# Order of the first loads, of the first panel's split and of the third panel's high part at the start of a two-block transformer kernel

## The reference, cut to what matters

```python
x = x + 0.5 * swiglu(rms_norm(x, norm_ffn1), ffn1_w1, ffn1_w3, ffn1_w2)

def swiglu(h, w1, w3, w2):
    return (jax.nn.silu(h @ w1) * (h @ w3)) @ w2

def rms_norm(x, g):
    xf = x.astype(jnp.float32)
    y = xf * lax.rsqrt(jnp.mean(xf * xf, axis=-1, keepdims=True) + EPS)
    return (y * g.astype(jnp.float32)).astype(x.dtype)
```

## Time and profile before

| | us |
|---|---|
| median of 3 runs | 2292.25 |
| lowest, highest of the 3 | 2291.9, 2292.46 |
| the profiled execution | 2291.65 |
| its span, first to last instruction | 2289.9 |

### The profile page before, as it was taken

The page is one execution under the profiler, slowest core; times in us unless marked ns, Lnnn a source line. Parts: engine busy times, 40 slices in busy tenths (PEclk is TensorE's granted clock), DMA queues, the critical chain, the costliest instruction groups (busy, mean ns, idle before and its releaser), DMA issues. The chain is left out here.

```text
span 2289.9 us, 35352 instructions
## 1 busy us (share of the span) xinstructions
PE 2235.4 (98%) x12536; PEld 1885.6 (82%) x12536; DVE 1122.1 (49%) x2070; ACT 1073.3 (47%) x2037; POOL 1161.0 (51%) x723
## 2 busy tenths in 40 slices
PE   7999999999999999999999999999999999999997
PEld 6999888777787789998877777677788887999986
DVE  4887425023441338884152688755511132787511
ACT  5555434145544555554333466644622234555433
POOL 3777457732272457774544522043344454676545
PEclk9999999999999999999999999999999999999998
DMA  4322334422221223323362211021122331333332
GB/s 174 111 98 104 94 101 146 120 74 72 67 92 56 83 75 110 103 99 99 96 155 77 83 38 47 10 77 62 47 92 92 94 108 63 100 104 110 91 94 92
DMA packets 81275, 206.59 MB, mean 90 GB/s; under 512 B 7440, under 2 KB 31120, under 8 KB 80912
## 3 DMA queue, kind: packets, MB, share of 16 engines
q1 hardware_dynamic: 72832, 191.92, 26.5%
q10 hardware_dynamic: 8336, 13.25, 2.1%
HBM read 199.71 MB, written 2.10 MB: 88 GB/s over the span
## 5 line engine op out<-in xcount | busy, mean ns | idle before, releaser
L680 POOL TENSOR_TENSOR parts<-slot,parts 128x512 fp32r<-128x512 f32 (+3 forms) x208 | 377.9, 1817 | 275.8 <-ACT parts L2280 274.0
L705 POOL TENSOR_TENSOR parts<-slot,parts 128x512 fp32r<-128x512 f32 x162 | 227.3, 1415 | 164.9 <-ACT parts L2339 161.8
L2280 ACT ACTIVATE parts<-slot 128x1024 fp32r<-128x1024 f32 (+2 forms) x170 | 154.1, 907 | 302.4 <-PE bank L914 253.0
L668 POOL TENSOR_TENSOR parts<-slot,lanes 128x1024 fp32r<-128x1024 f32 x42 | 80.8, 1924 | 237.8 <-PE bank L1817 115.7
L909 PE MATMUL bank<-hhi,parts 128*128 128x512 f32 x496 | 194.0, 391 | 2.8 <-POOL parts L680 2.7
L910 PE MATMUL bank<-hhi,parts 128*128 128x512 f32 x496 | 193.1, 389 | 0.0
L1080 PE MATMUL bank<-hhi,parts 128*128 128x256 f32 x756 | 188.7, 282 | 2.0 <-ACT sc L2383 2.0
L1081 PE MATMUL bank<-hhi,parts 128*128 128x256 f32 x756 | 189.0, 282 | 0.0
L677 POOL TENSOR_TENSOR parts<-slot,parts 128x512 fp32r<-128x512 f32 x55 | 71.3, 1296 | 220.2 <-ACT parts L2280 218.7
L1080 PEld LDWEIGHTS bank<-hhi,parts 128*128 128x128 f32 x756 | 144.1, 191 | 2.7 <-issue 2.5
L1081 PEld LDWEIGHTS bank<-hhi,parts 128*128 128x128 f32 x756 | 144.1, 191 | 0.1
(11 more groups left out here) (708 smaller groups left out, 6089.6 us busy)
## 6 DMA issues: line engine op xcount, KB each, us to landing
slot<-w SPq DMA_DIRECT2D x264, 512.0 KB, 3.6
slot<-w SPq DMA_DIRECT2D x88, 256.0 KB, 2.7
slot<-w SPq DMA_DIRECT2D x48, 448.0 KB, 3.2
hid<-w SPq DMA_DIRECT2D x8, 512.0 KB, 3.5
x<-xT ACTq DMA_DIRECT2D x4, 512.0 KB, 9.7
hid<-headtab ACTq DMA_DIRECT2D x8, 256.0 KB, 3.6
big<-cmpw ACTq DMA_DIRECT2D x4, 512.0 KB, 9.8
hid<-w SPq DMA_DIRECT2D x8, 256.0 KB, 2.5
```

The costliest lines, as they stand in the source:

```text
L668: pool.tensor_tensor(high, w, nought.unsqueeze(2).to_broadcast([P, KD, P]), ALU.add).then_inc(highs, 1)
L680: pool.tensor_tensor(low, w, high.bitcast(F32), ALU.subtract).then_inc(splits, 1)
L705: pool.tensor_tensor(low, source, high.bitcast(F32), ALU.subtract).then_inc(splits, 1)
L2280: act.activation(both(parts[nth % 2] if pair is None else pair)[0][:, 0:kt, :], slot[j][:, 0:kt, :], ACT.Copy).then_inc(highs, 1)
```

## The change

Five things change, all in the first 40 us of the program.

1. The second and fourth load of x (`x_loaded[1]` and `[3]`) go from ACT's queue into SP's, behind the first panel and ahead of the second. `memh`, `tables`, `gate_w` and `w2` go into SP's queue behind the fourth panel.
2. In ACT's queue stand `params`, the first and the third load of x, and then `consts`.
3. The first panel is split by halves of four k-tiles: ACT makes the high part of the first half as soon as the panel is there, the first `hhi` tile, then the high part of the second half. DVE, no longer POOL, makes both low parts. PE waits for the first half's low part, and for the second half's before its fifth k-tile.
4. The second panel's high part comes after the eight `hhi` tiles. POOL makes its low part alone, after the first panel's.
5. The third panel's high part comes after the second square and ahead of the third, no longer behind the root.

```diff
 # SP
                         sp.dma_start(slot[j][:, :, :], w8[panel[8] + j]).then_inc(loaded[j], 16)
+                        if phase == 0 and j == 0:
+                            for k in (1, 3):
+                                sp.dma_start(x[:, 2 * k:2 * k + 2, :], xT[:, 2 * k:2 * k + 2, :]).then_inc(x_loaded[k], 16)
+                    if phase == 0:
+                        sp.dma_start(memh[:, :, :], memT).then_inc(mem_loaded, 16)
+                        sp.dma_start(tables[:, :], tab).then_inc(tables_loaded, 16)
+                        sp.dma_start(gate_w[:, :, :], gatew).then_inc(gate_loaded, 16)
+                        sp.dma_start(w2[:, :], cmpw2).then_inc(cmp_loaded, 16)
...
 # POOL
             n.past(START)
-            for u in range(2):
-                ffn_split(u, n.at("highs"))
+            pool.wait_ge(splits, 1)
+            ffn_split(1, n.at("highs"))
...
 # PE, raw_high, called with by_halves for the first panel
-                pe.wait_ge(splits, n.at("splits", nth + 1))
+                if by_halves:
+                    pe.wait_ge(half_low, 1)
+                else:
+                    pe.wait_ge(splits, n.at("splits", nth + 1))
                 emptied(nth)
                 for k in range(KD):
+                    if by_halves and k == HK:
+                        pe.wait_ge(splits, n.at("splits", nth + 1))
...
 # ACT, the issues
             act.dma_start(params[:, :], par).then_inc(params_loaded, 16)
+            for k in (0, 2):
+                act.dma_start(x[:, 2 * k:2 * k + 2, :], xT[:, 2 * k:2 * k + 2, :]).then_inc(x_loaded[k], 16)
             act.dma_start(consts[:, :], con).then_inc(consts_loaded, 16)
-            for k in range(4):
-                act.dma_start(x[:, 2 * k:2 * k + 2, :], xT[:, 2 * k:2 * k + 2, :]).then_inc(x_loaded[k], 16)
-            act.dma_start(memh[:, :, :], memT).then_inc(mem_loaded, 16)
...
 # ACT, ffn_up
-                else:
+                elif not third_made:
                     high_part(2, 2, 1)
...
 # ACT, the start
+            act.wait_ge(loaded[0], 16)
+            act.activation(parts[0][:, 0, 0:HK, :], slot[0][:, 0:HK, :], ACT.Copy).then_inc(half_high, 1)
             act.wait_ge(params_loaded, 16)
-            for u in range(2):
-                high_part(u, u, None)
-            for k in range(KD):
+            act.wait_ge(x_loaded[0], 16)
+            raw_tile(0, G_FFN1)
+            act.activation(parts[0][:, 0, HK:KD, :], slot[0][:, HK:KD, :], ACT.Copy).then_inc(highs, 1)
+            for k in range(1, KD):
                 if k % 2 == 0:
                     act.wait_ge(x_loaded[k // 2], 16)
                 raw_tile(k, G_FFN1)
+            high_part(1, 1, None)
             for k in range(KD):
                 if k >= 2:
                     act.wait_ge(gsums, max(1, k - 2))
                 act.activation(sq[:, k % 2, :], x[:, k, :], ACT.Square).then_inc(squares, 1)
+                if k == 1:
+                    high_part(2, 2, 1)
...
 # DVE, the start
             dve.wait_ge(params_loaded, 16)
+            dve.wait_ge(half_high, 1)
+            dve.tensor_tensor(parts[0][:, 1, 0:HK, :], slot[0][:, 0:HK, :], parts[0][:, 0, 0:HK, :].bitcast(F32),
+                              ALU.subtract).then_inc(half_low, 1)
+            dve.wait_ge(highs, 1)
+            dve.tensor_tensor(parts[0][:, 1, HK:KD, :], slot[0][:, HK:KD, :], parts[0][:, 0, HK:KD, :].bitcast(F32),
+                              ALU.subtract).then_inc(splits, 1)
             for k in range(KD):
                 raw_low(k, G_FFN1)
```

15 lines of the change are left out of this document (6 added, 9 removed).

## The result

| | before | after |
|---|---|---|
| median, us | 2292.43 (7 runs) | 2299.68 (7 runs) |
| lowest, highest | 2290.11, 2293.61 | 2296.85, 2300.74 |
| ratio after / before, 95% interval | | 1.003, 1.0021 to 1.004 |
| profiled execution, us | 2291.65 | 2299.68 |
| its span, us | 2289.9 | 2297.9 |

The changed kernel is 7.25 us slower, 0.3%, between 4.8 and 9.2 us by the interval. The forecast was 0.5 us slower with a range of 2290.9 to 2294.6 us, and within 0.2%; the measured time lies outside of both.

What follows compares the result with a forecast made beforehand. PE, busy 98% of the span, was taken to bound the kernel; 0.4 us from a later first matmul plus 0.1 net behind it made 0.5 us slower, 2292.75 us, range 2290.9 to 2294.6.

Steps and rivals of the forecast that it cites:

- S: Time of PE's first matmul, set by the landing of `consts`; forecast 11.35 us, 0.4 later than before.
- The even shares: Start loads: ACT's and SP's queues share evenly when both move large loads, 0.22 and 0.20 MB per us.
- The 0.14 of rows 5: Profile rate, MB per us, of ACT's queue when `consts` was moving; gave 1.4 us for `consts`.
- The first product: First panel on PE: `hlo` tiles ready ahead of need, first product at S + 7.45, not S + 7.8.
- The third high part amid the squares: ACT, POOL and DVE at the squares: held additions bring the one-column matmuls 2.3 us later, at S + 14.75.
- DVE isn't held: Rival at the squares' additions: they run beside POOL, fourth panel 1.7 us earlier, 2291.05 us; chance 0.1.
- `consts` isn't late: Rival at the start: `consts` lands by 8, S about 8.3, fourth panel 2.1 us earlier, 2290.2 us; chance 0.1.
- The third and fourth panel: PE's third panel starts at S + 18.1 without its 2.71 us wait; the fourth waits 0.55, starts at S + 24.2.
- the clock rival: Clock falls in the new hole ahead of the one-column matmuls, slowing the third panel: 1.5 us more, 2294.3; chance 0.2.
- The difference is carried to the end unchanged: Behind the fourth panel each high part waits for PE's own products, so the start's difference stays the same.

Runs made afterwards that it cites:

- a_again: The changed kernel, unchanged, profiled a second time; time 2297.70 us, span 2295.9 us.
- a_fill400: The changed kernel with six more matmuls of no use ahead of the transposes at 411 us; median 2297.89 us.
- b_amid: The kernel before with only the third panel's high part moved between the second and the third square; median 2295.42 us.
- b_again2: The kernel before, unchanged, profiled a third time; time 2293.24 us.
- the mended one: The changed kernel, PE waiting for `consts` only at the one-column matmuls, third high part behind the last square; 2292.43 us, with six filler matmuls near 400 us 2290.95.
- a_fill: The changed kernel with twelve matmuls of no use in the hole ahead of the one-column matmuls; median 2296.61 us.
- a_warm: The changed kernel with twenty matmuls of no use ahead of PE's first, until `consts` has landed; median 2295.14 us.

## Why the prediction was wrong, point by point

**S: the right cause, the term too small.** `consts` set S as said, at 12.40 and 12.48 against 11.35. The even shares held while both queues had large loads. The term that failed is `consts` itself, "0.197 MB at 0.14, takes 1.4 us". ACT's and SP's queues of after, from 8 to 10 us and from 10 to 12: packets, MB, share.

```profile
q1 hardware_dynamic: 122, 0.43, 54.0%
q10 hardware_dynamic: 114, 0.39, 48.3%
```

```profile
q1 hardware_dynamic: 169, 0.63, 79.4%
q10 hardware_dynamic: 138, 0.18, 25.2%
```

The queues get near equal numbers of packets, not of bytes, and those of `consts` are small (192 KB over 128 partitions, 1.5 KB each): beside SP's large ones it got 0.09 MB per us, so 2.2 us for 0.197 MB by this estimate. That is 0.8 of the 1.05 us missed. The 0.14 of rows 5 was read as a rate of `consts`, but that stretch held more than `consts` and other neighbours. The Trainium skill, DMA: Bandwidth & Descriptors, section "Queues, rings and completion order", says that each DMA engine takes its queues in turn and drains a whole packet, of several descriptors, before it switches. The near equal counts fit taking turns; whether the profile's packets are those of the page no run here shows.

**The first product: the second panel 8.45 us after S in one profile, 7.16 in the other, forecast 7.15.** That DVE's `hlo` tiles are no longer late was right. Not in the sum at all was that the slow start has no fixed length: 14 slow matmuls in after and 8 in a_again are draws, worth 1.2 to 1.3 us (6.61 against 5.34 and 5.43 in a_again and a_fill400, which have the same start), and that the changed order lets them through to the third panel. The Trainium skill, TensorE: Matmul & The Clock Gate, Part 1, says the same of the start ("it's run-variable"); the prediction quoted that page's part and passed over this sentence.

**The third high part amid the squares: right.** The additions took 5.66 us because DVE was held (measured in after and alone in b_amid), PE's idle was 2.89 (forecast 3), and in a_again L954 stands at 27.23 = S + 14.75, as forecast. b_amid shows that this is a loss on its own. *DVE isn't held* and *`consts` isn't late* fell.

**The third and fourth panel: the first wait right, the pace wrong.** No wait ahead of the third, as said. The 0.55 us of wait ahead of the fourth isn't there, since the slow third panel used it up. S + 18.1 and S + 24.2 became S + 18.7 and S + 25.2 in a_again and S + 21.8 and S + 28.3 in after. The terms up to there and behind, us against before's first profile:

| | forecast | after | a_again |
|---|---|---|---|
| S | 0.38 | 1.43 | 1.51 |
| additions held by POOL | 2.29 | 2.29 | 2.29 |
| longer slow start | 0 | 1.29 | 0 |
| one-column matmuls to fourth panel, less 11.64 before | -2.19 | 0.59 | -1.21 |
| behind the fourth panel | 0 | 2.4 | 3.4 |
| end of the span | 0.5 | 8.0 | 6.0 |

**The failing step: the chance and the price of the fallen clock.** It is the largest miss in the table's column of after, 2.78 us in the fourth row (in that of a_again the fifth row's 3.4 is larger). The rival's mechanism was described with its place, and given 0.2. The argument against it was that before "kept the third panel at full pace" through its own hole. That was one execution; the same kernel lost its clock there in the next two. Twelve of thirteen profiles with such a hole have the fall, so its chance should have been near 0.9. The price, 1.5 us, was taken from a fall on dense matmuls behind the hole. From the one-column matmuls to the fourth panel the forecast had 9.45 us. It was 10.43 in a_again, 0.98 more, where the fall came late; and 12.23 in after, 2.78 more, where it came early and the sixteen one-column matmuls and the transposes, which stand on the path, ran slow too: 28.44 to 33.45 against 23.43 to 26.24 before.

But this step doesn't carry the 7.25 us alone. The kernel before pays for the fall too in most executions, so only a part of it is a difference between the two, and with the clock rival's own price the forecast would still have been 2294.3. The second step that failed is the next one, and behind it come S and the slow start.

**"The difference is carried to the end unchanged": wrong.** Behind the fourth panel it grew from 5.60 us to 8.0 in after, and between a_again and b_again2 from 1.07 to 4.5. In after nearly all of it comes at the transposes near 405 us: a hole longer by 0.62 us, and 3.49 us for sixteen transposes instead of 1.94 because the clock fell in them. The longer hole is there in all nine profiles of the changed order, the fall in six. That filling it saves time (1.8 us in the changed kernel, 1.5 in the mended one) is likely, but within the intervals. How the start's order reaches DVE's instructions 370 us later was not followed.

**The range.** It was built from one profile plus bounds on two waits. The single runs of before alone go from 2289 to 2295, which three runs within 0.6 us had not shown. The seven runs of the changed kernel, 2296.85 to 2300.74, all lie above them, so the miss is no luck of one run.

**What stays open:** how the loss divides between the parts. Undone one at a time they give back 5.1, 3.5 and 2.9 us, done alone they cost 1.8 and 2.8, with 4.7 for the rest, each to about 2 us. The three are the whole change, so together they are the 7.25; their shares are not shown, and they overlap, since the one wait that was seen in the rest, the second panel's 1.33 us behind a high part that comes after all `hhi` tiles, isn't there in the changed kernel with its late `consts`.

## What to carry to other kernels

Before moving an operation ahead of its place, ask what is queued behind it, on its own engine and on the engine that its helper holds up: here the third high part won 3 us behind the last square and lost 3 six squares earlier. Before costing a hole, profile the kernel more than once: a hole that kept its clock in one execution lost it in the next two, and a difference of a few us between two single profiles can be such a draw. A small load queued behind large ones came late here, and put ahead of them it made the next one late; what helped most was to wait for it only at its first use.

## What the runs showed of the hardware that I had not expected

- The granted clock behind one and the same hole of 2.7 us stayed at 2.4 GHz in one execution of the kernel before and fell to 1.2 GHz in two, which moved the fourth panel by 1.5 to 1.7 us. With the hole filled it could still fall (a_fill, at 31.2).
- From one start order the slow first stretch lasted until 18.5 us in one execution and 16.0 in another. In the changed kernel that delayed the one-column matmuls in full (1.21 us); in the kernel before up to 0.94 us of it came out as 0.2 there.
- Twenty matmuls whose result nobody reads, run while PE would wait for a load, made the kernel 4.5 us faster (a_warm): the slow stretch then lay in time that was idle anyway.
- A load of 0.197 MB in packets of 1.5 KB went at 0.09 MB per us, in a stretch (10 to 12 us in after) in which the queue beside it, with larger packets, got 0.32.
- A change in the first 40 us went with a longer hole 370 us later: 2.25 us or more in nine of nine profiles, where the kernel before and its variants had 1.64 to 1.69 in five of six. By what way was not shown.
